# The recurrence of a hybrid trunk layer: another order of score jobs, key turns and chain chunks within a period

## The reference

```python
def step(S, xs):
    r_t, w_t, k_t, v_t, a_t, b_t = xs
    sa = jnp.einsum('bhvk,bhk->bhv', S, a_t)
    S = S * w_t[:, :, None, :] + sa[..., None] * b_t[:, :, None, :] + v_t[..., None] * k_t[:, :, None, :]
    return S, jnp.einsum('bhvk,bhk->bhv', S, r_t)
```

## Time and profile before

| what | value |
|---|---|
| three runs | 3092.06, 3084.24, 3091.88 us; median 3091.88 |
| the profiled execution's own time | 3092.32 us |
| its span, first to last instruction | 3090.6 us |
| mean granted TensorE clock of it | 0.933 of full speed |
| recurrence, PE's first to last matmul | 1003.1 to about 1557 us |

### The profile page before, as it was taken

How to read it: one execution, slowest core, us unless ns; L and a number is a source line. 1 busy time by engine, 2 the same in 40 slices (tenths; PEclk the granted TensorE clock), 3 DMA queues, 4 the chain that set the end, 5 groups by cost and what they waited for, 6 DMA issues and landing times. The chain is left out here.

```text
span 3090.6 us, 60845 instructions
## 1 busy us (share of the span) xinstructions
PE 2733.2 (88%) x25988; PEld 1566.4 (51%) x25988; DVE 1371.1 (44%) x2369; ACT 521.6 (17%) x1459; POOL 450.0 (15%) x639
## 2 busy tenths in 40 slices
PE   5799999999867588989866999999999999999993
PEld 1467676666546588888833444333333333333320
DVE  1667576767365455555363121533222323222323
ACT  1100000000044355555310121100000000000001
POOL 0100000000064455454120000000000000000000
PEclk8799999999979699999878999999999999999996
DMA  9576645555276312111058778799999999999997
GB/s 409 202 224 201 211 161 198 194 198 186 81 204 119 114 40 64 46 41 42 21 208 287 282 284 310 310 409 400 388 403 404 404 404 398 394 405 405 406 413 275
DMA packets 268517, 783.60 MB, mean 254 GB/s; under 512 B 99473, under 2 KB 163112, under 8 KB 199712
## 3 DMA queue, kind: packets, MB, share of 16 engines
q1 hardware_dynamic: 257104, 724.13, 62.3%
q0 software_dynamic: 10848, 56.51, 6.2%
q10 hardware_dynamic: 368, 0.10, 0.0%
HBM read 712.59 MB, written 68.08 MB: 253 GB/s over the span
## 5 line engine op out<-in xcount | busy, mean ns | idle before, releaser
L2207 PE MATMUL oe_ps<-experts_ring,tail_arena 128*32 128x512 f32 x4096 | 503.7, 607 | 42.4 <-DMA experts_ring<-in_w_up 39.7
L478 DVE SCALAR_TENSOR_TENSOR pj_macc<-pj_mring,head_cond_t,pj_macc 128x1024 f32<-128x1024 f32 x240 | 297.3, 1281 | 182.1 <-DMA pj_mring<-in_w_ada 182.1
L2207 PEld LDWEIGHTS oe_ps<-experts_ring,tail_arena 128*32 128x32 f32 x4096 | 152.8, 112 | 340.8 <-issue 339.9
L551 PE MATMUL pj_ps<-head_hT,head_ring_in 128*128 128x320 f32 x1104 | 313.6, 437 | 5.9 <-DVE head_hT L451 3.5
L2240 PE MATMUL oe_ps<-experts_ring,oe_hidt 128*32 128x512 f32 x2880 | 312.0, 592 | 0.0
L2215 PE MATMUL oe_ps<-experts_ring,tail_arena 128*32 128x512 f32 x2048 | 274.2, 602 | 0.0
L551 PEld LDWEIGHTS pj_ps<-head_hT,head_ring_in 128*128 128x128 f32 x1104 | 211.9, 192 | 96.1 <-DVE head_hT L451 6.3
L2544 DVE SCALAR_TENSOR_TENSOR oe_hid_s<-oe_hid_s,oe_gcol_s,oe_ps 128x512 f32<-128x512 f32 x16 | 12.0, 747 | 535.2 <-ACT oe_hid_s L2390 535.2
L2286 PE MATMUL oe_ps<-experts_ring,tail_arena 128*128 128x512 f32 x520 | 232.8, 605 | 14.4 <-DMA tail_arena<-scratch_o 14.4
L551 PE MATMUL pj_ps<-pj_t,pj_s 128*128 128x320 f32 x736 | 209.3, 438 | 6.1 <-DVE pj_t L457 6.1
L2240 PEld LDWEIGHTS oe_ps<-experts_ring,oe_hidt 128*32 128x32 f32 x2880 | 108.0, 110 | 201.0 <-issue 201.0
(11 more groups left out here) (411 smaller groups left out, 3916.6 us busy)
## 6 DMA issues: line engine op xcount, KB each, us to landing
experts_ring<-in_w_gate SPq DMA_DIRECT2D x128, 1024.0 KB, 23.8
experts_ring<-in_w_up SPq DMA_DIRECT2D x128, 1024.0 KB, 25.5
experts_ring<-in_w_down SPq DMA_DIRECT2D x128, 1024.0 KB, 22.3
experts_ring<-in_w_out SPq DMA_DIRECT2D x68, 1024.0 KB, 6.9
pj_mring<-in_w_ada SPq DMA_DIRECT2D x64, 1024.0 KB, 9.6
head_ring_in<-in_w_in SPq DMA_DIRECT2D x23, 2048.0 KB, 7.7
ada_ring<-in_w_ada SPq DMA_DIRECT2D x16, 2048.0 KB, 18.9
scratch_z<-pj_stage POOLq DMA_DIRECT2D x19, 640.0 KB, 8.2
```

The source lines that it names most:

```text
L478: a = nc.vector.scalar_tensor_tensor(acc, w, scalar, acc, ALU.mult, ALU.add)
L551: mm = pe.matmul(bank(name, b)[:, 0:TH], a[:, k, :], h[:, k, :], start=(k == 0), stop=(k == KH - 1))
L2207: pe.matmul(ps[32 * i:32 * i + 32, bank, :], xe[:, k, GROUPS[i % 2]], w[:, kk * DE + 512 * (i // 2):kk * DE + 512 * (i // 2) + 512], start ...
```

## The change

The score jobs are cut anew. Before, job b held chunks 2b and 2b+1 with both kinds of keys. After, jobs 0 and 1 hold the removal keys' blocks of chunks 0 to 3 and 4 to 7, job 2 both kinds for chunks 8 and 9, and jobs 3 and 4 the keys' blocks of chunks 0 to 3 and 4 to 7. `blocks_out` and `halve` wait for job 2 where they waited for job 4 (`halve` for the job with its last chunk). Jobs 3 and 4 and the second job of turned keys go to the late part, the two turns and the first "x" jobs come after job 2, and `CUTS` gives the late part six chunks and the early part four. The order after, for an even u:

```diff
--- before.py
+++ after.py
@@ -1136,8 +1136,11 @@
     SB = 8
     FIRST_LV, LAST_LV = 2, 4
     LEVELS = range(FIRST_LV, LAST_LV + 1)
-    CUTS = (2, 5, 7)
+    CUTS = (3, 5, 8)
     STEPS = 2 * (SB - 2)
+    SCORES = [[(c, 0) for c in range(4)], [(c, 0) for c in range(4, 8)], [(c, j) for c in (8, 9) for j in range(2)],
+              [(c, 1) for c in range(4)], [(c, 1) for c in range(4, 8)]]
+    LAST_B = 2
     MOVED, ZEROS = 5 * 16, NT * 16
     HALF = T // 2
     ORDER = [list(range(NCK)), list(range(NCP))[::-1] + list(range(NCP, NCK))[::-1]]
@@ -1154,16 +1157,18 @@
         bk = [("bk", b, u) if now else None for b in range(2)]
         lv = {(kind, b, n): (kind, b, n, u - 1) if 1 <= u <= NU else None for kind in ("x", "d") for b in range(2) for n in LEVELS}
         turns = ["turn0", "turn1"] if 1 <= u <= NU else []
-        items = [w0, a0, w1, a1, s0, "slot", sc[0], "scan", "slot", sc[1], *turns, lv["x", 0, 2], "slot", sc[2], lv["x", 1, 2], "slot", "removal", sc[3], lv["d", 0, 2], "slot",
-                 sc[4], lv["d", 1, 2], "slot", "exp_in", lv["x", 0, 3], "slot", bk[0], lv["x", 1, 3], "exp_inv", "slot", "pad_b", lv["d", 0, 3], "slot", "half0", lv["d", 1, 3],
-                 "exp_ex", "slot", "half1", "pad_k", lv["x", 0, 4], "slot", "decay", bk[1], lv["x", 1, 4], "slot", "far", lv["d", 0, 4], "slot", "pad_a", lv["d", 1, 4]]
+        items = [w0, a0, w1, a1, s0, "slot", sc[0], "scan", "slot", sc[1], "slot", sc[2], *turns, "slot", lv["x", 0, 2], "slot", lv["x", 1, 2], "slot", "removal",
+                 lv["d", 0, 2], "slot", lv["d", 1, 2], "slot", "exp_in", lv["x", 0, 3], "slot", bk[0], lv["x", 1, 3], "exp_inv", "slot", "pad_b", lv["d", 0, 3], "slot", "half0",
+                 lv["d", 1, 3], "exp_ex", "slot", "half1", "pad_k", lv["x", 0, 4], "slot", "decay", lv["x", 1, 4], "slot", "far", lv["d", 0, 4], "slot", "pad_a", lv["d", 1, 4]]
         return kept_items(u, items)
 
     def late(u):
 
         now = u < NU
         vt = [("vt", b, u) if now and u % 2 == 0 else None for b in range(2)]
-        return kept_items(u, ["slot", ("bk", 2, u) if now else None, "slot", vt[0], "slot", vt[1], "slot"])
+        sc = [("sc", b, u) if now else None for b in (3, 4)]
+        bk = [("bk", b, u) if now else None for b in (1, 2)]
+        return kept_items(u, ["slot", sc[0], "slot", bk[0], "slot", sc[1], "slot", bk[1], "slot", vt[0], "slot", vt[1], "slot"])
 
     def kept_items(u, items):
 
@@ -1292,7 +1297,7 @@
 
             def blocks_out(u):
 
-                sp.wait_ge(dve_ev, RANK[G["sc", NCK // 2 - 1, u]])
+                sp.wait_ge(dve_ev, RANK[G["sc", LAST_B, u]])
                 sp.wait_ge(moved, ZEROS + MOVED * u)
                 for h in range(2):
                     sp.dma_start(lb_d[h, 0:CK * NCK * CK].rearrange("(s c t) -> s c t", s=CK, t=CK), sc[HEADS[h], u % NS, :, 0, 0:CK]).then_inc(moved, 16)
@@ -1495,11 +1500,8 @@
                     pe.wait_ge(bkp_done, 2 * u + 2)
                     pe.wait_ge(pad_done, u + 1)
                     pe.wait_ge(rb_done, u + 1)
-                    for i in range(2):
-                        c = 2 * b + i
-                        for j in range(2):
-                            mm = heads(bank[:, (2 * i + j) * P:(2 * i + j + 1) * P], bk[:, u % 2, j * NCK + c, :],
-                                       aq[:, u % NQ, c].rearrange("p i t -> p (i t)"), True, True)
+                    for n, (c, j) in enumerate(SCORES[b]):
+                        mm = heads(bank[:, n * P:(n + 1) * P], bk[:, u % 2, j * NCK + c, :], aq[:, u % NQ, c].rearrange("p i t -> p (i t)"), True, True)
                 else:
                     if kind == "x" and key[2] != LAST_LV - 1:
                         pe.wait_ge(halved, 3 * u + (3 if key[2] == LAST_LV else b + 1))
@@ -1590,7 +1592,7 @@
 
             def halve(u, dst, c0, c1, other):
 
-                act.wait_ge(dve_ev, RANK[G["sc", (c1 - 1) // 2, u]])
+                act.wait_ge(dve_ev, RANK[G["sc", LAST_B, u]])
                 if u:
                     act.wait_ge(job, G["x", 1, LAST_LV if other else LAST_LV - 1, u - 1] + 1)
                 for h in range(2):
@@ -1682,7 +1684,9 @@
                 bank = rot[:, G[key] % R]
                 dve.wait_ge(job, G[key] + 1)
                 if kind == "sc":
-                    nc.vector.tensor_tensor(sc[:, u % NS, 2 * b:2 * b + 2].rearrange("p c i n -> p (c i) n"), bank.rearrange("p (i n) -> p i n", n=2 * CK),
+                    (c0, j0), (c1, j1) = SCORES[b][0], SCORES[b][-1]
+                    to = sc[:, u % NS, c0:c1 + 1].rearrange("p c i n -> p (c i) n") if j0 != j1 else sc[:, u % NS, c0:c1 + 1, j0, :]
+                    nc.vector.tensor_tensor(to, bank.rearrange("p (i n) -> p i n", n=2 * CK),
                                             mask[:, d:d + 1, :].to_broadcast([P, 4, 2 * CK]), ALU.mult).then_inc(dve_ev, 1)
                     return
                 lv = key[2]
```

## The result

After: 3094.78 us, the median of ten runs (3087.91 to 3101.54). Before, on the same chip: 3086.64, the median of ten (3083.48 to 3092.84). The ratio is 1.0027 with a 95% interval of 1.0014 to 1.0039; a second series gave 1.0024 [1.0012, 1.0037]. The change makes the kernel slower by about 8 us, where 13 us faster was forecast. The time lies inside the forecast's range (3060 to 3105), but on the other side of no change than the forecast.

A forecast was written before the change was run, and what follows sets the result against it. The prediction took PE's stream with its waits as the bound of a period, DVE's order making the largest wait. Start -3, periods -2 and clock -8 gave -13 us on 3092.3: 3079 us, range 3060 to 3105.

The forecast's parts named there:

- Start: Start of the recurrence: the first store waits for job 2, so the string behind it comes 3.2 us earlier, once.
- First wait of a period: PE's wait for the turned block before the first inversion job: from 2.04 to 1.1 us, 0.95 less a period.
- Waits that come up in its place: Early part, before x03, x04 and d04: the inversion's own latency shows, 1.3 us more a period.
- Late part: Late part of a period: fillers leave 1.0 us of waits in three steps where 1.4 stood, 0.4 less.
- Clock: PE's clock drops in ten periods, 1.6 us each: half of the 16 us comes back, 8 us less.
- drops as many as now: Rival on PE's clock: the period is only reordered and drops stay, 3087 us; chance 0.28.
- the slower one: Rival: the inversion stretch runs at 1.2 GHz twice as long, 3.2 us a period, 3119 us; chance 0.16.
- all drops go: Rival on PE's clock: every drop vanishes, 16 us back, 3071 us; chance 0.23.

The follow-up runs named there:

- r_before: The kernel before, run once more unchanged for a second profile: 3087.98 us.
- r_after: The changed kernel, run again unchanged for a second profile: median 3090.06 us, ratio 1.0024 to the kernel before; its profiled execution took 3096.70 us.
- e8: The changed kernel with its cuts set back to (2, 5, 7), so new score jobs and moved jobs only: 3054.61 us, 0.9914 of before.
- e7: The kernel before with new score jobs, early store and cuts (3, 5, 8), but its old order of jobs: 3073.60 us, 0.9968 of before.
- e11: The changed kernel with cuts (2, 5, 8), five chunks in the late part in place of six: 3075.05 us, 0.9966 of before.
- e12: The changed kernel with unneeded products filling three waits (two before x02, one each before x03 and x04): 3074.05 us, 0.9963 of before.
- e3: The kernel before with three unneeded products in PE's wait before x02: 3063.35 us, 0.9931 of before.
- e2: The kernel before with only the cuts changed, from (2, 5, 7) to (3, 5, 8): 3072.76 us, 0.9960 of before.
- e1: The kernel before with only the new score jobs and the earlier store, order and cuts as before: 3072.80 us, 0.9969 of before.
- e6: The changed kernel with two unneeded products in its first wait, before x02: 3091.20 us, 1.0029 of before.

## Why the prediction went wrong

The sum was -13 us. The medians say +8, and the second pair of traces, by which I go here, +9.7 in the recurrence: 22.7 us are to be explained. The steps, one by one, with signs for the time:

- *Start*, -3.2 forecast, -1.6 measured (51.60 to 49.99). The store and the read behind it came 3.7 us earlier, more than forecast, and POOL no longer waits for the read, so the elimination starts 3.8 us earlier (31.55 to 27.75 us into the recurrence). But its first three instructions take 1.5 us longer there than in r_before (2.92 to 1.40, from the first start to the fourth), and three score jobs instead of two now stand before x02, 0.8 us. The step took it that the whole string moves with its first link. r_before, then r_after:

```profile
1040.38 0.40 POOL L1395 TENSOR_TENSOR rw_prod<-rw_blk 16x60 f32<-16x60 f32 x1 [3.67 <-DMA rw_blk<-scratch_lb]
...
1035.51 0.99 POOL L1400 TENSOR_TENSOR rw_prod<-rw_blk 16x60 f32<-16x60 f32 x1
1036.58 0.80 POOL L1402 TENSOR_TENSOR rw_blk<-rw_blk,rw_prod 16x60 f32<-16x60 f32 x1
```

- *First wait of a period*, 2.04 to 1.1 forecast; 1.06 measured. Right, with its cause.
- *Waits that come up in its place*, +1.3 forecast with 0.85 before x04 and 0.25 before x03. Measured 0.73 and 0.47. The early part got 4.35 us shorter (16.37 to 12.02) for 5.57 us of products moved out (three score jobs 2.64, a keys job 0.94, 17 groups 1.99), so +1.22 in all. Right.
- *Late part*, -0.4 forecast. **This is the term that failed in the period.** It got 5.12 us longer (5.34 to 10.46) for 4.7 us of products moved in (two score jobs 1.76, a keys job 0.94, 17 groups 2.0), which makes +0.4 of waits. The idea of fillers was right as far as it went: with two steps and the move, e8's late part holds 7.21 us for about 6.6 of products, 0.6 of waits where before has 1.4. But the third step brings 1.2 to 1.3 us of its own, as e7, e8 and e11 show, and I had given the three steps 1.0 together. Against the forecast that is 0.8 us a period. The periods were to be 2 us shorter in all (0.05 a period is 0.8 us; the rounding made 2 of it) and are 9.7 us longer, as e12 against e3 shows: 11.7 us off.
- *Clock*, -8 forecast. In the twelve periods it is 15.9 to 19.5, +3.6. **This is the other term that failed.** My price of before's drops, 16 us, was right. The change has fewer drops (eight in r_after's twelve periods, ten in r_before's), but seven of them last 6.8 us and not 3.4. Two of the seven begin within 2.3 us of the wait before x02, five after the wait before x04, and these run on into the late part. That is 11.6 us off. The first two periods are 5.5 us longer beside: the second is 7.0 longer, with two spells of 6.8 us where r_before has none (34.40 against 27.38), the first 1.5 shorter.
- Not in the sum at all: the fifteenth period and the tail, -7.6 us together. Fewer chunks are left over at the end when more are done in each late part, and e2 and e7 have tails of 40.8 and 41.4 us. But that is not all of it, as e1, with before's cuts, has 43.3: r_before waits 2.40 us before its last x02, e1, e2 and r_after not at all, and the tail's clock is 0.77 in r_before and 0.82 in r_after. So 1.6 + 11.7 + 11.6 + 5.5 - 7.6 makes 22.8.

Of the rivals, "drops as many as now" gave the clock's share best, and the slower one had its place right and its size too large: the spells do start in the inversion stretch and do last twice as long, but in seven periods of twelve, not in all, and such a spell costs 2.3 to 2.8 us, not 3.2 (r_after: 32.17 and 31.63 us for an odd period that is 29.37 without).

The Trainium skill ("TensorE: Matmul & The Clock Gate", section "HAM oscillation — how this bites in real kernels") ascribes the falls to idle gaps between bursts. The traces agree that far: with the gaps filled there is no drop in twelve periods, in either order. But the gaps it describes are waits for loads, longer than any in these periods, and here the clock falls behind waits of 2.04 us and less. Nor did halving the wait bring the drops to an end, as the rival "all drops go" had it: before x02 it went from 2.04 to 1.06, and with waits of 1.06, 0.47 and 0.73 us within some 10 us the clock falls in fewer periods and for longer. The section "A second HAM failure mode: psum-queue depth-cycling" of the same page says that frequent short idles make the gate swing. e6 and e12 agree with it: filling one of the three did nothing, filling all three gave 19 us.

Open stays what exactly waits in the third late step. In the late part of after no single wait is over 0.2 us in the timeline, so it must be a sum of small ones; which, no run took apart. Open is also why the drops in e2 cease with 1.57 us of wait in every period: the size of the waits alone does not tell where the clock falls.

## What to carry to other kernels

Where PE waits for one engine's in-order list, look first at what stands ahead of the awaited instruction in that list: letting DVE turn before it scans gave 1.3%, more than the best of the change's parts (jobs and move, 0.9%) or products that fill the wait (0.7%). Work between dependent jobs covers their waits. Moving it away cost at both ends here (0.9 us back for 1.6 taken out, 3.25 spent for 2.0 put in), and two steps that each gain can lose together (jobs and move 0.86%, cuts 0.40%, all three -0.24 to -0.27%), so measure them in pairs. And price a reordering at full clock and in drops separately: a handful of unneeded products in each wait makes the two visible.

## What the runs showed of the hardware

- A spell at half clock of 3.4 us costs 1.6 us (30.30 against 28.70), one of 6.8 us costs 2.3 to 2.8: less than twice as much.
- Unneeded products paid for themselves: 21 us less in before and 19 in after, for three or four of them in a period. In e12 they lengthen a period by 0.1 us at full clock (29.45 against 29.35).
- The same 505 products of the first period took 31.73 us (before and r_before) or 24.45 (e1), with no difference but which blocks each job makes and the waits between: at a mean granted clock of 0.68 or 1.00.
- PE can be busy all through and stay at 1.2 GHz: 6.83 of 6.83 us in after, in the inversion stretch.
- The clock fell in ten of twelve periods with one wait of 2.04 us (r_before), in eight with waits of 1.06, 0.47 and 0.73 (r_after), and in none of the last eight with waits of 1.57 and 0.23 (e2).
